# Norm and head factors by quarters of the tokens, the first norm by token, and another cut of the projections

## The reference

```python
def rms_norm(x, gain):
    y = xf * lax.rsqrt(jnp.mean(xf * xf, axis=-1, keepdims=True) + EPS)
    return (y * gain.astype(F32)).astype(x.dtype)

def l2_norm(x):
    return (xf * lax.rsqrt(jnp.sum(xf * xf, axis=-1, keepdims=True) + EPS)).astype(x.dtype)

h = modulate(rms_norm(x, norm_mix), sh_m, sc_m)            # the first norm, and one more before the MLP
(qa, ka, va, qb, kb, vb, qkv_c, z_c, beta_c, a_c, gate) = jnp.split(h @ w_in, IN_OFFSETS, axis=-1)
...
qkv = short_conv(qkv, conv_w)                              # branch C: five taps, SiLU
q = l2_norm(heads(q, C_HEADS)); k = l2_norm(heads(k, C_HEADS))     # 4 heads of 128 each
gc = jnp.cumsum(chunks(g), axis=-1)                        # log decays, cumulated in chunks of 64
...
x = x + gt_m * merge_branches(o_a, o_b, o_c, gate, w_branch, w_out)
x = x + gt_f * sq_relu_mlp(modulate(rms_norm(x, norm_ffn), sh_f, sc_f), w_ffn1, w_ffn2)
```

## Time and profile before

| | |
|---|---|
| median of 3 runs | 3140.11 us (3133.85 to 3140.86) |
| the profiled execution | 3130.7 us, span of the trace 3128.8 us |
| busy: PE, PEld, DVE, ACT, POOL | 94%, 79%, 41%, 34%, 33% of the span |
| mean granted clock of TensorE | 0.979 of full speed |
| read from HBM, mean | 217 MB, 73 GB/s over the span |

### The profile page before, as it was taken

How to read it: one execution, slowest core, us unless ns; L and a number is a source line. 1 busy time by engine, 2 the same in 40 slices (tenths; PEclk the granted TensorE clock), 3 DMA queues, 4 the chain that set the end, 5 groups by cost and what they waited for, 6 DMA issues and landing times. The chain is left out here.

```text
span 3128.8 us, 57462 instructions
## 1 busy us (share of the span) xinstructions
PE 2927.5 (94%) x24851; PEld 2476.6 (79%) x24851; DVE 1270.1 (41%) x1795; ACT 1055.1 (34%) x1770; POOL 1043.8 (33%) x704
## 2 busy tenths in 40 slices
PE   5998898998899999899999989999999999989997
PEld 4887787886678887788888877788787788778886
DVE  4874343245641113422222268654245721252223
ACT  4542222225542112322222245533225532333222
POOL 3234344220313333222323222354430344434443
PEclk8899999999999999999999999999999999999999
DMA  6116453110012232122122221100310034323331
GB/s 235 58 31 205 138 191 109 54 54 1 12 31 63 63 101 68 47 64 65 61 68 61 68 75 54 49 3 3 88 51 12 12 101 132 98 80 95 101 94 68
DMA packets 303691, 231.94 MB, mean 74 GB/s; under 512 B 16784, under 2 KB 275280, under 8 KB 302544
## 3 DMA queue, kind: packets, MB, share of 16 engines
q1 hardware_dynamic: 297360, 204.58, 21.8%
q0 software_dynamic: 3776, 17.91, 1.6%
q10 hardware_dynamic: 2304, 5.77, 0.5%
HBM read 217.22 MB, written 11.98 MB: 73 GB/s over the span
## 5 line engine op out<-in xcount | busy, mean ns | idle before, releaser
L1789 POOL TENSOR_TENSOR wl<-wring,wh 128x1024 fp32r<-128x1024 f32 (+1 forms) x312 | 725.3, 2327 | 1355.2 <-ACT wh L1060 1352.8
L433 PE MATMUL ps<-hh,wh 128*128 128x512 f32 (+1 forms) x2392 | 855.4, 358 | 20.2 <-DVE hl L1691 11.2
L434 PE MATMUL ps<-hl,wh 128*128 128x512 f32 (+1 forms) x2392 | 840.1, 351 | 0.0
L435 PE MATMUL ps<-hh,wl 128*128 128x512 f32 (+1 forms) x2392 | 839.5, 351 | 0.0
L433 PEld LDWEIGHTS ps<-hh,wh 128*128 128x128 f32 x2392 | 454.6, 190 | 91.6 <-DVE hl L1691 14.5
L434 PEld LDWEIGHTS ps<-hl,wh 128*128 128x128 f32 x2392 | 454.8, 190 | 64.7 <-issue 5.1
L435 PEld LDWEIGHTS ps<-hh,wl 128*128 128x128 f32 x2392 | 454.0, 190 | 61.0
L1060 ACT ACTIVATE wh<-wring 128x1024 fp32r<-128x1024 f32 (+1 forms) x312 | 307.7, 987 | 497.8 <-PE ps L435 487.9
L1719 DVE SCALAR_TENSOR_TENSOR R<-ps,modcs,R 128x512 f32<-128x512 f32 x216 | 136.3, 659 | 361.8 <-PE ps L435 361.4
L434 PE MATMUL ps<-fl,wh 128*128 128x512 f32 (+1 forms) x768 | 272.4, 355 | 0.0
L433 PE MATMUL ps<-fh,wh 128*128 128x512 f32 (+1 forms) x768 | 272.1, 354 | 0.0
(11 more groups left out here) (244 smaller groups left out, 3907.2 us busy)
## 6 DMA issues: line engine op xcount, KB each, us to landing
wring<-in_w_ffn SPq DMA_DIRECT2D x128, 512.0 KB, 3.7
wring<-in_w_in SPq DMA_DIRECT2D x116, 512.0 KB, 3.6
wboth<-in_w_mod SPq DMA_DIRECT2D x80, 512.0 KB, 6.3
wring<-in_w_branch SPq DMA_DIRECT2D x48, 256.0 KB, 2.6
wring<-in_w_out SPq DMA_DIRECT2D x16, 512.0 KB, 4.0
x_store<-R POOLq DMA_DIRECT2D x2, 3072.0 KB, 9.7
R<-x_store POOLq DMA_DIRECT2D x2, 3072.0 KB, 10.9
R<-in_w_mod SPq DMA_DIRECT2D x7, 512.0 KB, 12.6
```

The lines of the kernel that those rows point to most:

```text
L433: mm(ps[:, t0:t1], ahk, rh[:, k, t0:t1], start=(k == 0), stop=False)
L434: mm(ps[:, t0:t1], ahk, rl[:, k, t0:t1], start=False, stop=False)
L435: last = mm(ps[:, t0:t1], alk, rh[:, k, t0:t1], start=False, stop=(k == kn - 1))
L1789: G.tensor_tensor(slot_view(wl, n % NSPL, l, name, i), w, slot_view(wh, n % NSPL, l, name, i).bitcast(F32), ALU.subtract)\
```

## The change

- Sums for the roots are made on quarters of the tokens (`quarter_sums`): quarter g of the columns goes to partitions 32g to 32g+31, by four products with 32 columns of ones. Root and reciprocal then run over 192 (or 128) columns instead of 768 (or 512). `spread` brings a quarter back to all 128 partitions by a product whose weights are one column of the identity, repeated. This holds for the three later norms, the final one, and the head factors of branch C (new buffers `csp`). VectorE reads the factors from PSUM; for the final norm ScalarE also copies them out.
- In the convolution stage the spread of a head block stands one step behind its sums, and its scaling (`head_scaled`) at the head of the next step on VectorE.
- The first norm is made by token: ScalarE squares each x tile as it lands, with the sum in the same instruction; root and reciprocal run over six columns; six products with the identity turn them into a row on all partitions. VectorE now copies the transposed x out.
- The first 16 pieces of `w_mod` no longer go through `wring`: pieces 0 to 2 have homes at the end of `hh`. The first three projection weights are loaded behind piece 6 of SyncE's own; ScalarE issues its eight pieces behind the second square.
- Cumulative sums: one product for all six tiles, so 5 instead of 30.
- Projections with 768 tokens are cut at column 496 instead of 512 (`CUT`), and land at column 16 of the buffer, so that the first 496 columns fill up the first bank and 272 follow in the second.
- Parameters of layer 1 are loaded later and turned at p = 4; the wait for `spilled` goes from VectorE's clearing to ScalarE's step p = 3.

```diff
+CUT = 496
...
+        def runs(n):
+            return ((0, CUT), (CUT, TOK)) if n == TOK else ((0, n),)
+        def landing(n):
+            return LAT - CUT if n == TOK else 0
+        def landed(n, *key):
+            return pair(*key)[:, landing(n):landing(n) + n]
+        def spread_at(n):
+            return LAT - n // 2
...
             def project(key, w, ntok, rhs=None, kn=KC, m0=0, ready=None, ps=None, done=True):
-                ps = take(pe, *key)
-                for t0, t1 in ((0, LAT), (LAT, TOK))[:1 if ntok == LAT else 2]:
+                ps = take(pe, *key)[:, landing(ntok):landing(ntok) + ntok]
+                for t0, t1 in runs(ntok):
...
+            def quarter_sums(ps, sq, n, start=True, stop=True):
+                w = n // 4
+                for g in range(4):
+                    last = mm(ps[32 * g:32 * g + 32, 0:w], ones[:, 0:32], sq[:, g * w:g * w + w], start=start, stop=stop)
+                return last
+            def spread(ps, rows, n):
+                w, c0 = n // 4, spread_at(n)
+                for g in (0, 2, 1, 3):
+                    lo = HALF * (g // 2)
+                    pick = ident[lo:lo + HALF, 32 * g:32 * g + 1].to_broadcast([HALF, P])
+                    last = mm(ps[:, c0 + g * w:c0 + g * w + w], pick, rows[lo:lo + HALF, 0:w], start=True, stop=True)
+                return last
...
             def norm(l, which, ntok):
-                    for t0, t1 in ((0, LAT), (LAT, TOK))[:1 if ntok == LAT else 2]:
-                        last = mm(ps[:, t0:t1], ones, sq[:, t0:t1], start=(k == KC - 3), stop=(k == KC - 1))
-                last.then_inc(*filled("ss", l, which))
+                    last = quarter_sums(ps, sq_n[:, 0, :] if k == KC - 3 else square_home(k), ntok,
+                                        start=(k == KC - 3), stop=(k == KC - 1))
+                last.then_inc(*pe_done.mark("ss", l, which))
+                pe.wait_ge(*dve_done.at("rs", l, which))
+                spread(ps, rs_n, ntok).then_inc(*filled("ss", l, which))
...
-                    norm(0, "mix", TOK)
                     params(0)
+                    pe.wait_ge(*dve_done.at("rs0"))
+                    ps = take(pe, "ss", 0, "mix")
+                    for t in range(TT):
+                        last = mm(ps[:, t * P:t * P + P], small[:, 16 + t:17 + t].to_broadcast([P, P]), ident,
+                                  start=True, stop=True)
...
-                        for t in range(TT):
-                            b = 32 * t
-                            mm(ps[:, b:b + 4], cst[:, C_UI:C_UI + P], gt[:, t, 0:4], start=True, stop=True)
...
+                        mm(sums[:, :, 0:4], cst[:, C_UI:C_UI + P], gt[:, :, 0:4], start=True, stop=True)
+                        mm(sums[:, :, 4:8], cst[:, C_LI:C_LI + P], gt[:, :, 4:8], start=True, stop=True)
+                        mm(sums[:, :, 8:16], blk, gt[:, :, :], start=True, stop=True)
...
+                    if p >= 4 and c_order[p - 4] < 8:
+                        head_spread(l, c_order[p - 4])
                     if p >= 3 and c_order[p - 3] < 8:
...
-                        for t0, t1 in ((0, LAT), (LAT, TOK))[:1 if conv_cols(l, j) == LAT else 2]:
-                            last = mm(ps[:, t0:t1], ones, csq[:, j % 2, t0:t1], start=True, stop=True)
+                        quarter_sums(take(pe, "css", l, j), csq[:, j % 2, :], conv_cols(l, j)).then_inc(*filled("css", l, j))
...
             def inverse_root(l, which, ntok):
-                V.reciprocal(rs_n[:, 0:ntok], rs_n[:, 0:ntok]).then_inc(*dve_done.mark("rs", l, which))
+                V.reciprocal(rs_n[:, 0:ntok // 4], rs_n[:, 0:ntok // 4]).then_inc(*dve_done.mark("rs", l, which))
...
+            for t in range(TT):
+                act.wait_ge(*x_in[t].at())
+                A(hl_head[:, :], r(S0 + 1024 * t, 1024), ACT.Square, accum_out=small[:, t:t + 1])\
+                    .then_inc(*act_done.mark("xsq", t))
+                if t == 1:
+                    for i in range(1, 16, 2):
+                        act.dma_start(mod_home(i), mod_slot(0, i)[4][0][2]).then_inc(*mod_in[i].mark(by=16))
...
-                dve.wait_ge(*spilled.at(l))
...
+                    if p == 3:
+                        act.wait_ge(*spilled.at(l))
```

More of the change, by code:

```diff
@@ L333, in plan @@
         def plan():
-            for i in range(NRAW):
-                yield mod_slot(0, i)
             for l in range(DEPTH):
@@ L992, in square @@
             def square(l, which, ntok, k):
[L994 to L998 removed]
+                act.wait_ge(*(read("out", l, k) if which == "ffn" else read("ff2", l - 1, NG - 1, k)))
                 if k in (4, 5, 7):
@@ L1069, in _ @@
                 nt = TOK if l == 0 else LAT
[L1070 to L1075 removed]
+                if l:
                     high(l, "c", c_order[0], ahead=1)
[L1077 removed]
+                norm(l, "mix", TOK, first=KC if l == 0 else 6)
                 def decays(l):
@@ L1357, in norm @@
                     return
+                if (l, which) != (0, "mix"):
+                    rs = pair("ss", l, which)[:, spread_at(ntok):spread_at(ntok) + ntok]
                 w = int(which == "ffn")
@@ L1360, in norm @@
                 for k in range(KC + 1):
+                    if k == KC and (l, which) != (0, "mix"):
+                        dve.wait_ge(*dve_done.at("scaled", l, which, KC - 1))
+                        V.memset(small[:, 61:62], 0.0).then_inc(*free("ss", l, which))
                     if k < KC and k >= 3:
@@ L1466, in params @@
                         dve.wait_ge(*read("params", ll))
-                    for k in range(1, KC - 2):
-                        square_sum(0, "mix", TOK, k)
-                    inverse_root(0, "mix", TOK)
+                    for t in range(TT):
+                        dve.wait_ge(*full("x", t))
+                        V.tensor_copy(xT[:, :, t * P:t * P + P], pair("x", t)[:, :].rearrange("p (k n) -> p k n", k=KC))\
+                            .then_inc(*free("x", t))
+                    dve.wait_ge(*act_done.at("root0"))
+                    V.reciprocal(small[:, 16:16 + TT], small[:, 8:8 + TT]).then_inc(*dve_done.mark("rs0"))
                     params(0)
@@ L1793, in normed @@
             def normed(l, which, ntok, ks):
-                pool.wait_ge(*dve_done.at("rs", l, which))
+                pool.wait_ge(*read("ss", l, which))
                 for k in ks:
```

154 lines of the change are left out of this document (85 added, 69 removed).

## The result

Timed on one chip, the changed kernel took 3101.12 us (median of 4 runs, 3098.97 to 3105.42) against 3140.49 before (4 runs, 3133.85 to 3141.53). The ratio is 0.9885 with a 95% interval of 0.9868 to 0.9902: 39 us, or 1.2%, faster. The forecast was 3074. The direction was right and the range held, but 27 us of the 66 forecast did not come. The measured time is also, by coincidence, the 3101 of rival A; A took it from a cut that gives nothing, and the cut gave 13 us (e1).

The account below looks back on a forecast made before the run. TensorE, busy 94% of the span, was taken to bound the kernel. Terms of -27-15.6-9.4-0.5-13 = -65.5, taken as -66 us, from the median 3140.1 gave 3074 us, range 3047 to 3108.

Parts of the forecast that it names:

- rival A: Projections: the cut gives nothing, products costing columns at 2.4 GHz plus 0.0133 us; 3101 us, chance 0.19.
- Step 1: Projections with 768 tokens: cutting at 496+272 instead of 512+256 columns saves 27 us, between ends of nothing and 30.
- A rate and a floor: Projection products: 0.443 ns a column, with a floor of 0.120 us per instruction from the weight load beside the product.
- Step 2: Kernel start: first projection product at 45 us instead of 60.65, a gain of 15.6 us, ends 10 and 19.
- 35 us, with the smaller pieces 38: Start: time when w_mod's load ends, 14.2 MB at 407 GB/s, then with the first 2 us and smaller weight pieces.
- Step 3: Cumulative decays in the convolution stage: 5 products instead of 30 save 4.7 us a layer, 9.4 in all, ends 5 and 13.
- Step 4: Head factors in the convolution stage: quartered sums and spread give about -0.5 us in sum, VectorE's shorter reciprocal nothing.
- Rival B: Convolution stage: TensorE waits for the factors before every spread, 2 us on 16; 3106 us, chance 0.06.
- Step 5: Later and final norms: -4.2 us twice at 768 tokens, -2.7 at 512, -2.1 final; together -13, ends -8 and -15.

Follow-up runs that it names:

- e1: Changed kernel with the cut alone undone (512 and 256 columns again): 3112.48 us, ratio 0.9927 to the kernel before.
- e3: Changed kernel with the projections cut into two equal halves of 384 columns: 3101.21 us, ratio 0.9898 to the kernel before.
- e7: Changed kernel with w_mod's last four tiles issued behind the first projection weight instead of the third: 3101.05 us, one run, against 3133.50 before.
- e11: Kernel before with only the cumulative decays changed, 5 products in place of 30: 3135.46 us against 3138.24, ratio 1.0001.
- e6: Changed kernel with the cumulative decays as 30 small products again: 3118.64 us, one run, against 3133.50 for the kernel before.
- e4: Changed kernel with VectorE's copy of gcs moved ahead of the head scaling and convolution of its step: 3089.44 us, ratio 0.9853 to the kernel before.
- e5: e4 with head factors on the whole width again (sums, root, reciprocal over all columns, scaling in the same step): 3097.34 us, ratio 0.9901 to the kernel before.

## Why the prediction was right, and where 27 us of it went

**Step 1, the cut: mis-sized, -13 measured for -27.** "A rate and a floor" was wrong: 384 columns cost 0.1733, not 0.170 (e3). The trace of before held 226.67 and 120.0, and both are columns at 2.4 GHz plus 0.0133, the rule that I had as rival A. I argued against it with the 0.02 us behind runs of short products. That loss was real and is gone after, and it is one part of the gain (0.020 per projection over the rule); the other part is that 272 columns come 0.003 cheaper than the rule. By exact distances 0.100 is saved on a kn=8 and 0.060 on a kn=4 projection, against 0.18 and 0.10 on record: 120 x 0.100+88 x 0.060 = 17 us where nothing waits, and 13 in the timed runs, since the projections of the convolution stages gain next to nothing (e1's stages there: 0.6 longer and 0.3 shorter than after), and since a stretch that falls on the dear price gains nothing either (three of twelve did). The forecast had neither. The long product was forecast to the nanosecond (0.2196, measured 0.2200), the short one was 0.003 off, and 3936 of those are 12 us.
The Trainium skill, TensorE: Matmul & The Clock Gate, section Back-to-back issue gap, has for a single product columns by the clock plus 2.5 ns: 384+384 agrees in form but not in the constant, which is 13.3 ns here (0.1733 = 0.1600+0.0133). The cut by that rule would have saved nothing, and e1 measures 13; the measurement decides.

**Step 2, the start: -11.7 for -15.6.** The chain from the gains on took the 3.7 us forecast (1.15+2.55) and measured 3.7 (48.91-45.22). The term that failed is "35 us, with the smaller pieces 38": w_mod landed at 41.41, 3.4 late, and from there to the gains it took 3.5 for 2.9. Between the last x tiles and the first w_mod tile next to nothing moves for a slice of 1.25 us (44 GB/s, some 400 on either side), and two more weight tiles, issued at 36.26 and 38.57, load beside the last w_mod tiles; how the 3.4 divide between them was not measured. e7 shows that the last w_mod tiles land 2.76 earlier when two weight tiles stand behind them, and that this order gains nothing. The lock of VectorE and GpSimd that the forecast took from the Trainium skill (SBUF — State Buffer, section SBUF: two separate sides) shows again in e7, 5.14 us beside splits of 5.09, where after it isn't met at all.

**Step 3, the decays: right in every row, and still wrongly put.** Ten issues in 1.14, a wait for `gcs` of 6.95 for the 5 forecast, 3.9 and 4.1 us less from projection to projection for 4.7; then 9.7 and 9.8 us for the next projection instead of 8.9 and 8.4 before, at the lower clock, so 3.0 and 2.8 net. But that is not what the five products bring. Alone they bring nothing (e11), beside the quartered factors they bring 9.6 and 9.4 (e6).

**Step 4, the head factors: here the working failed.** It said of VectorE's shorter reciprocal: "its cover is that VectorE is off the path here, so that gives nothing". It was off the path only as long as 30 small products stood before it. The four corners, in us of layer 0's convolution stage (all versions but before and e11 have the new cut, start and norms too; the cut is 0.6 of it, by e1; - is not run):

```
                         30 products     5 products
whole width              179.4 (before)  181.0 (e11)
quarters                 187.2 (e6)      177.7 (after)
quarters, gcs first      -               168.7 (e4)
whole, gcs first         -               177.3 (e5)
```

The quarters alone cost 7.8 us: the PSUM buffer that their spread takes puts the wait for `gcs` on the path (6.06 us in e6, none before). Together with the products they turn into a gain, and with that wait gone, they are worth 8.6 in layer 0 and 4.5 in layer 1. That VectorE's reciprocal carries this gain, and not something else that comes with whole factors, rests on the rows of e5, where VectorE is busy without a gap up to the keys that TensorE waits for; no run changed the reciprocal alone. On TensorE the block became 0.2 (768 columns) to 0.36 (512) dearer instead of 0.2 cheaper: the spread takes 0.85 from its start to the next one's, and the sums 0.47, 1.3 together for the 1.10 of before. So 0.4 to 0.55 a block was off the working, 6 us over 14 blocks, beside the decays' 1.7 and 1.9; some 2 us of both came back in the stages' first head block, where TensorE waits 2.5 us for squares instead of 3.5.
Rival B, a wait before every spread, didn't come: in the changed kernel no spread of these stages waits over 0.02 us.

**Step 5, the other norms: -11.4 for -13.** From the start of the last sums to the first product 3.7, 3.5, 2.0 and 2.2 us were saved, for 4.2, 4.2, 2.7 and 2.1. The spread at the lower clock took most of the difference (1.50 for 0.8).

**Not in the sum: layer 1's delta stage, +4.6.** It shows in every version that has quarters in the convolution stage and five products, and in neither e5 nor e6; e11, with five products alone, has 1.6 us of it. After, four stretches of its first step:

```profile
1968.00:1972.00 4.00, 2.97 (x16) 1.32 (x16) 1.13 (x4) 2.96 (x7) 2.32 (x4) 0.77 0.68 264
1972.00:1976.00 4.00, 2.10 (x36) 1.50 (x32) 2.17 (x4) 1.50 (x4) 3.32 (x4) 0.80 0.01 4
1976.00:1980.00 4.00, 2.69 (x48) 2.40 (x50) 2.96 (x5) 0.66 (x2) 3.83 (x5) 0.62 0.00 0
1980.00:1984.00 4.00, 4.00 (x84) 4.00 (x82) 1.98 (x4) 0.77 (x2) 0.61 (x1) 0.52 0.00 0
```

The granted clock falls to 0.52; before it stayed at 1.00 at this place, though TensorE idled nearly as much: 4.1 us of 16 from 1992 on, 4.9 here from 1964 on. The stage ahead ends with a spread and 1.7 us of idling (before: 1.6, without a spread). What tips it isn't settled.

**The sum.** Cut -13, start -11.7, norms -11.4, the two convolution stages -2.8 beside their part of the cut, layer 1's delta stage +4.6: -34, where the timed runs say -39 with an interval of 5 to either side. Against the record the cut misses 14 us, steps 3 and 4 together 7, the start 4 and the norms 2, which are the 27; the 4.6 come on top and lie within the interval. The two traces say -25: the profiled execution of before, 3130.7, was faster than all four timed ones, that of the changed kernel the slowest of its four. 5.2 us of the difference are in the delta stage of layer 0, and 2 in the cut, which is 11 by the traces; what the rest is stays open.
That the range held is in part luck: the measured time lies 7 us inside its slow end, and of the five terms the largest was twice too large and the head factors rested on a cover that did not last. The forecast also added its part 4 loosely: 14 x 0.2 less and 2.8 more at the stages' ends make 0, not -0.5.

## What to carry to other kernels

That an engine is off the path holds only for the cover it has now. Where one edit takes small work off the bound engine and another shortens the chain on the engine beside it, price the four corners: here each alone gives nothing or costs 8 us, and the two together, with one copy moved, give 10 a layer in the traces' convolution stages.
Two sizes of a product don't tell a rate with a floor from a rate with a constant. Look for a third size, between or beyond, before the sum rests on either. And look at the distances in more than one execution: one trace showed one of two prices.
When a step takes one more buffer of a rotating set, find who frees the one four takes back, and put that reader first on its engine: moving one copy of 0.35 us was worth 10 us of the kernel.

## What the runs showed of the hardware that I had not expected

Long fp32r products cost the same for 504 and 512 columns (0.2275 and 0.2278 us) and for 488 and 496 (0.2197 and 0.2200), each by one trace. After a run of 256-column products the first 512s lose 0.02 us in all; 496s behind 272s lose nothing in nine long stretches, and 0.06 to 0.10 a projection in three others, at a granted clock of 1.00 in the one shown. In its cheap stretches the pair of 496 and 272 is 1% cheaper than 384 and 384; that of 480 and 288 is 1% dearer.
While w_mod is loaded in bursts (up to 374 GB/s over 8 us in the changed kernel) TensorE idles at small products without a wait that the profile names, 15.7 us in a stage of 273. With half of the bytes gone the stage is 29 us shorter: 17 less idle time, and 12 less busy time at a clock of 0.99 for 0.96.
A GpSimd split beside VectorE's scalings stretched them from 1.15 to 5.14 us (e7); the same pair stood in rows 5.
